# Six FFNs take the second half of x through memory and VectorE and interleave two groups' halves; span levels paired, entry reordered

## What is computed

```python
x = x + 0.5 * swiglu(rmsnorm(x, ffn1_norm), wg, wu, wd)     # D_FF = 2816
h = rmsnorm(x, mix_norm)
x = x + mixing(h @ w_in) @ w_out
x = x + 0.5 * swiglu(rmsnorm(x, ffn2_norm), ...)
...
def swiglu(h, w_gate, w_up, w_down):
    return (jax.nn.silu(h @ w_gate) * (h @ w_up)) @ w_down
```

## Time and profile before

| | |
|---|---|
| median of three runs | 1969.18 us |
| the profiled execution | 1967.95 us |
| its span, first to last instruction | 1966.1 us |
| PE busy | 1953.5 us, 99% |
| DVE busy | 1368.3 us, 70% |
| ACT busy | 1048.3 us, 53% |
| DMA, mean | 202 GB/s |
| matmul records of line 477 with 512 columns | 3 x 1552 and 3 x 832 |
| transposes of x at line 522 | 176 |
| transposes of `act` at line 636 | 68 |
| granted TensorE clock, mean share | 0.999 |

### The profile page before, as it was taken

One profiled execution on the slowest core, in us unless ns is written; L12 is line 12 of the kernel. 1 busy time (PEld: TensorE's weight loads), 2 busy tenths in 40 slices (PEclk: granted clock), 3 DMA queues, 4 the chain that ended last, 5 costly groups with the idle time before them and its releaser, 6 DMA issues.

```text
span 1966.1 us, 27227 instructions
## 1 busy us (share of the span) xinstructions
PE 1953.5 (99%) x11122; PEld 1643.0 (84%) x11122; DVE 1368.3 (70%) x1690; ACT 1048.3 (53%) x1326; POOL 39.5 (2%) x73
## 2 busy tenths in 40 slices
PE   9999999999999999999999999999999999999998
PEld 7888988888888888888888898788888889878887
DVE  6666986666666697666666679766666667976665
ACT  5545675445544657544644466654454446765444
POOL 0120003000000000000000000000000000000000
PEclk9999999999999999999999999999999999999999
DMA  8765546665666544566566644356656664435662
GB/s 321 256 229 193 167 156 217 227 225 193 216 226 225 188 164 169 214 225 218 188 225 228 217 171 160 142 199 225 224 188 235 224 226 161 171 136 194 227 226 78
DMA packets 146749, 396.77 MB, mean 202 GB/s; under 512 B 82128, under 2 KB 100816, under 8 KB 104128
## 3 DMA queue, kind: packets, MB, share of 16 engines
q1 hardware_dynamic: 144704, 390.90, 57.3%
q0 software_dynamic: 1488, 3.78, 0.6%
q10 hardware_dynamic: 432, 0.35, 0.1%
HBM read 372.97 MB, written 19.66 MB: 200 GB/s over the span
## 4 chain that ended last, share of the span: by engine, by line
PE 91%; DVE 5%; ACT 2%; DVEq 1%; issue 1%; DMA 1%; ACTq 0%; SPq 0%
PE bank L477 86%; DVE w_lo L1423 2%; PE bank L522 1%; DMA x<-xt 1%; PE bank L711 1%; PE bank L831 0%; PE bank L727 0%; ACT w_hi L992 0%; PE bank L850 0%; PE bank L636 0%; PE bank L744 0%; PE bank L812 0%; PE bank L700 0%; DVE arena L1561 0%; PE bank L788 0%
## 5 line engine op out<-in xcount | busy, mean ns | idle before, releaser
L1423 DVE TENSOR_TENSOR w_lo<-raw,w_hi 128x2048 fp32r<-128x2048 f32 x330 | 756.2, 2292 | 385.0 <-ACT w_hi L992 384.5
L992 ACT ACTIVATE w_hi<-raw 128x2048 fp32r<-128x2048 f32 x330 | 629.5, 1909 | 247.4 <-PE bank L477 244.9
L477 PE MATMUL bank<-w_hi,h_hi 128*128 128x512 f32 x1552 | 608.5, 392 | 1.9 <-DVE w_lo L1423 1.9
L477 PE MATMUL bank<-w_hi,h_lo 128*128 128x512 f32 x1552 | 604.4, 389 | 0.0
L477 PE MATMUL bank<-w_lo,h_hi 128*128 128x512 f32 x1552 | 604.1, 389 | 0.0
L477 PEld LDWEIGHTS bank<-w_hi,h_hi 128*128 128x128 f32 x1552 | 291.3, 188 | 65.1 <-DVE w_lo L1423 3.2
L477 PEld LDWEIGHTS bank<-w_hi,h_lo 128*128 128x128 f32 x1552 | 291.3, 188 | 61.0
L477 PEld LDWEIGHTS bank<-w_lo,h_hi 128*128 128x128 f32 x1552 | 291.4, 188 | 59.4
L477 PE MATMUL bank<-w_hi,act_hi 128*128 128x512 f32 x832 | 326.8, 393 | 0.0
L477 PE MATMUL bank<-w_hi,act_lo 128*128 128x512 f32 x832 | 324.1, 390 | 0.0
L477 PE MATMUL bank<-w_lo,act_hi 128*128 128x512 f32 x832 | 323.9, 389 | 0.0
(11 more groups left out here) (242 smaller groups left out, 1352.1 us busy)
## 6 DMA issues: line engine op xcount, KB each, us to landing
raw<-stream SPq DMA_DIRECT2D x331, 1024.0 KB, 4.9
spill<-scratch SPq DMA_DIRECT2D x71, 256.0 KB, 3.6
scratch<-spill SPq DMA_DIRECT2D x71, 256.0 KB, 2.7
arena<-arena SPq DMA_DIRECT2D x32, 64.0 KB, 2.7
arena<-rpb POOLq DMA_DIRECT2D x16, 66.5 KB, 4.2
x<-xt SPq DMA_DIRECT2D x1, 1024.0 KB, 12.8
arena<-final_gain POOLq DMA_DIRECT2D x2, 512.0 KB, 5.4
out<-x SPq DMA_DIRECT2D x3, 256.0 KB, 2.5
```

The source lines that it names most:

```text
L477: last = mm(o, a, r, start=start and n == 0, stop=stop and n == len(pairs) - 1)
L992: fn(w_hi[u % SLOTS][:, :], raw[u % RAW][:, :], ACT.Copy).then_inc(hi_done, 1)
L1423: tt(w_lo[u % SLOTS][:, :], raw[u % RAW][:, :], w_hi[u % SLOTS][:, :].bitcast(F32), ALU.subtract).then_inc(lo_done, 1)
```

## The change

It touches the six FFNs other than the first of each model (`SWAPPED`).

- x's second half of columns isn't transposed by PE. When a piece of it is updated, SP writes it to memory (`spill_x`, 256 KB, pieces of 64 columns), waits for both, and reads both back in another order of partitions (`swap_x`). This stands in SP's list behind the raw load of the unit that is five places behind the FFN's first one. DVE transposes 32 x 32 blocks, two instructions of 128 x 256 for each quarter (`x_turn`). The rows of the gate and up weights and of the norm's gain are permuted on the host to match (`swapped_rows`).
- PE's order is front 0, front 1, back 0, first tile of back 1, turn of `act` 0, second tile of back 1, down 0. The stream has places 1 and 2 exchanged for this.
- DVE's order at the entry: updates and h_lo of quarters 0 and 1, split of front 1, sum of squares, split of back 0, two turns of x, h_lo of quarters 2 and 3, splits of places 3 and 4, gates. ACT's: squares and h_hi of quarters 0 and 1, root, split of back 0 and place 3, h_hi of quarters 2 and 3, split of place 4, gates.
- Span levels 0 and 1, and in model 1 also 2 and 3, stand in one slot, the later one, and the second of each pair uses the banks `PD[2:4]` and, for level 3 of model 1, a scaled tile of its own. In model 2 the split of unit 7 moves behind the eviction of unit 5.
- At the kernel's entry quarters 2 and 3 are split together ahead of unit 1, and unit 2 is split in halves.

```diff
+SPANS_AT = [{3: (0, 1), 5: (2, 3), **{t + 2: (t,) for t in range(4, 9)}}, {6: (0, 1), **{t + 5: (t,) for t in range(2, 9)}}]
+SECOND = [(1, 3), (1,)]
+SWAPPED = [(b, L, j) for b in range(2) for L in range(LAYERS) for j in range(2) if (L, j) != (0, 0)]
+SWAPPED_NORMS = [3 * (2 * b + L) + 2 * j for b, L, j in SWAPPED]
...
+        x_landed, x_columns = part(7168, 2, 512), part(8192, 4, T)
-        PS = banks[:, 2:4, :]
+        qks_second = decay_A[:, 0, :, :].rearrange("p (a b) t -> p a b t", a=2)
...
+                if (b, L, j) in SWAPPED and off in (1, 2):
+                    off = 3 - off
...
+        def scaled_tile(b, t):
+
+            return qks2 if b == 1 else qks_second if t == 3 else qks1
+
+        def span_banks(b, t):
+
+            return 4 if t in SECOND[b] else 2
...
+            elif nn in SWAPPED_NORMS and i >= 2:
+                engine.wait_ge(x_turned, 2 * SWAPPED_NORMS.index(nn) + i - 1)
             else:
-                engine.wait_ge(xt_ready, 4 * (nn - 1) + i + 1)
+                engine.wait_ge(xt_ready, sum(2 if m in SWAPPED_NORMS else 4 for m in range(1, nn)) + i + 1)
...
+            if nn in SWAPPED_NORMS and i >= 2:
+                return x_columns[:, 2 * (i - 2) + c, :]
...
+            def swap_x(b, L, j):
+
+                no = SWAPPED.index((b, L, j))
+                for t in range(2):
+                    wait_x(sp, x_no(b, L, 2 * j), 2 + t)
+                    sp.dma_start(spill_x[t].rearrange("c p h -> p c h"), x[:, t, 512:D].rearrange("p (c h) -> p c h", c=8)).then_inc(x_out, 16)
+                sp.wait_ge(x_out, 32 * (no + 1))
+                for t in range(2):
+                    sp.dma_start(x_landed[:, t, :].rearrange("p (q n) -> p q n", q=2),
+                                 spill_x[t].rearrange("(q c) (r a) h -> (c r) q (a h)", q=2, a=4)).then_inc(x_back, 16)
...
-            exchanged = {ffn_use(b, L, j, "front", g) + SLOTS + RAW: (b, L, j, g) for b, L, j, g in EXCHANGED}
+            exchanged = {ffn_use(b, L, j, "back", g) + SLOTS + RAW - 1: (b, L, j, g) for b, L, j, g in EXCHANGED}
+            swapped = {ffn_use(b, L, j, "front", 0) + RAW: (b, L, j) for b, L, j in SWAPPED}
...
+                if u in swapped:
+                    swap_x(*swapped[u])
...
+                if following is not None and nn + 1 not in SWAPPED_NORMS:
...
+                        if g == 0 and kk == 0 and u > 0 and nn not in SWAPPED_NORMS:
...
+                        if t == 0 and between is not None:
+                            between()
...
                 front(PD, 0)
-                back(PD, 0)
-                for g in range(1, GROUPS):
+                if nn in SWAPPED_NORMS:
+                    front(PB, 1)
+                    back(PD, 0)
+                    back(PB, 1, lambda: turn_act(0))
+                    down(0)
+                else:
+                    back(PD, 0)
+                for g in range(2 if nn in SWAPPED_NORMS else 1, GROUPS):
                     front(PB, g)
...
-                if t >= 1:
-                    pe.wait_ge(span_copied, base)
-                src = (qk1, qk2)[b] if kind == "diag" else (qks1, qks2)[b]
+                if t >= 2:
+                    pe.wait_ge(span_copied, base - (t in SECOND[b]))
+                src = (qk1, qk2)[b] if kind == "diag" else scaled_tile(b, t)
...
-                if i in SPAN_AFTER[b]:
-                    span_step(b, L, SPAN_AFTER[b][i])
+                for t in SPANS_AT[b].get(i, ()):
+                    span_step(b, L, t)
...
+                swap = (b, L, j) in SWAPPED
+                if swap:
+                    squares(v, [0, 1])
+                    turned_hi(b, L, 2 * j, [0, 1])
+                    squares(v, [2, 3])
+                    root(v)
+                    split(use_of("back", 0))
+                    split(use_of("front", 0) + SLOTS)
+                    turned_hi(b, L, 2 * j, [2, 3])
+                    split(use_of("front", 1) + SLOTS)
+                elif v > 0:
...
-                    for half in range(2):
-                        turned_hi(b, L, 2 * j, [half + 2])
-                        half_high(1, half)
-                    split(use_of("front", 1))
+                    turned_hi(b, L, 2 * j, [2, 3])
+                    for u in (1, 2):
+                        for half in range(2):
+                            half_high(u, half)
...
-                root(x_no(b, L, 2 * j))
-                if v > 0 and not entry:
-                    split(use_of("front", 1))
+                if not swap:
+                    root(x_no(b, L, 2 * j))
-                if not late:
-                    split(use_of("front", 0) + SLOTS)
...
-                    split(use_of("front", g) + SLOTS)
+                    if not (swap and g == 1):
+                        split(use_of("front", g) + SLOTS)
...
+                def x_turn(b, L, j, q):
+
+                    dve.wait_ge(x_back, 32 * (SWAPPED.index((b, L, j)) + 1))
+                    for t in range(2):
+                        v.transpose(x_columns[:, 2 * q:2 * q + 2, :].rearrange("p k (t r a) -> p t a k r", t=2, a=4)[:, t],
+                                    x_landed[:, t, 256 * q:256 * q + 256].rearrange("p (a k i) -> p a k i", a=4, k=2))
+                    dve.drain().then_inc(x_turned, 1)
...
+                swap = (b, L, j) in SWAPPED
+                if swap:
+                    update(nn - 1, (0.5, 1.0)[j], [0, 1, 2])
+                    turned_lo(b, L, 2 * j, [0])
+                    update(nn - 1, (0.5, 1.0)[j], [3])
+                    turned_lo(b, L, 2 * j, [1])
+                    split(use_of("front", 1))
+                    mean_square(at)
+                    split(use_of("back", 0))
+                    for q in range(2):
+                        x_turn(b, L, j, q)
+                    turned_lo(b, L, 2 * j, [2, 3])
+                    split(use_of("front", 0) + SLOTS)
+                    split(use_of("front", 1) + SLOTS)
...
-                    for half in range(2):
-                        turned_lo(b, L, 2 * j, [half + 2])
-                        half_low(1, half)
-                    split(use_of("front", 1))
+                    turned_lo(b, L, 2 * j, [2, 3])
+                    for u in (1, 2):
+                        for half in range(2):
+                            half_low(u, half)
...
-                if at > 0 and not entry:
-                    split(use_of("front", 1))
                 late = entry or at == 0
-                if not late:
-                    split(use_of("front", 0) + SLOTS)
...
-                    split(use_of("front", g) + SLOTS)
+                    if not (swap and g == 1):
+                        split(use_of("front", g) + SLOTS)
...
-                    tt(qks1.rearrange("p a b t -> p (a b t)"), qk1.rearrange("p a b t -> p (a b t)"),
+                    tt(scaled_tile(0, t).rearrange("p a b t -> p (a b t)"), qk1.rearrange("p a b t -> p (a b t)"),
...
-                src = PS[:, :, 0:T].rearrange("p o (n t) -> p o n t", t=64)
+                at = span_banks(b, t)
+                src = banks[:, at:at + 2, 0:T].rearrange("p o (n t) -> p o n t", t=64)
...
-                split(mix_use(1, L, 7))
...
+                    if b == 1 and i == 5:
+                        split(mix_use(1, L, 7))
...
-                    if t < len(STEPS) and not (b == 0 and i == RECURRENCE_AFTER[b]):
-                        span_copy(b, L, t)
+                    if not (b == 0 and i == RECURRENCE_AFTER[b]):
+                        for done in SPANS_AT[b].get(i, ()):
+                            span_copy(b, L, done)
...
+def swapped_rows(w):
+
+    half = w[512:].reshape(2, 4, 2, 32, -1).transpose(0, 2, 1, 3, 4).reshape(512, -1)
+    return np.concatenate([w[:512], half], 0)
...
+                if (b, L, j) in SWAPPED:
+                    g, u = ([swapped_rows(w[L])] * LAYERS for w in (g, u))
+                at = len(out)
...
+                if (b, L, j) in SWAPPED:
+                    out[at + 1], out[at + 2] = out[at + 2], out[at + 1]
...
+            norms = [i[n + tail][L].reshape(D, 1) for n in ("ffn1_norm", "mix_norm", "ffn2_norm")]
+            norms = [swapped_rows(w) if (b, L, n // 2) in SWAPPED and n != 1 else w for n, w in enumerate(norms)]
```

More of the change, by code:

```diff
@@ L88, in build @@
 def build(nc, stream, xt, x_cols, params, final_gain, code_w, gate_w, forget_w, rpb,
-          lower, positions, forget_bias, c_square, c_level, c_col, c_att, c_freq, c_sel, c_reset, spill, out):
+          lower, positions, forget_bias, c_square, c_level, c_col, c_att, c_freq, c_sel, c_reset, spill, spill_x, out):
     ctx = ExitStack()
@@ L538, in last_row_unit @@
                         turn(nn + 1, x, 0, 1)
-                if following is not None:
+                if following is not None and nn + 1 not in SWAPPED_NORMS:
                     wait_x(pe, following, 2)
@@ L617, in front, with back @@
                     last.then_inc(used, 1)
-                def back(banks, g):
```

(12 more changed lines are left out.)

11 lines of the change are left out of this document (5 added, 6 removed).

## The result

The changed kernel takes 1972.05 us (median of 21 runs, 1971.26 to 1973.85), the kernel before 1969.01 in 21 runs beside it: ratio 1.0017, 95% interval 1.0010 to 1.0023. That is +3.0 us where +0.6 was forecast: inside the range and inside the 0.2% (3.9 us) called no change, but the interval leaves out 1, so the kernel is slower, by 0.10 to 0.23%. The direction of the forecast (what is gained is spent on a new wait) stands; its size is 2.4 us short.

The account below looks back on a forecast made before the run. PE's issue rate bounds the kernel (busy 1953.5 of 1966.1 us). Six FFN entries +1.8, paired span levels -1.2, model 2's pairs 0 and the kernel's entry 0 make +0.6 on 1969.18: 1969.8 us, range 1965.3 to 1976.

Parts of the forecast that it names:

- The transposes ahead of front 0: FFN entries: this group takes 0.49 us but only fills the wait for h_lo; priced at nothing, bound 0.08 us.
- Those inside front 0, 0.43 us: FFN entries: removing the four transposes inside the first unit gains 0.35 us plus 0.08 of restart.
- The chain to back 0: FFN entry: root 789.94, w_lo 792.61 to 794.81, x's columns 793.9; DVE's order, not the DMAs, sets the time.
- ACT's h_hi ... is ready at 796.85, so DVE makes h_lo from 797.07: FFN entry, after the turn: h_lo ready 797.95, PE starts 798.1, waiting 0.7 us ahead of back 0.
- net +0.3 us at each entry: Six FFN entries: back 0 ends at 803.6 instead of 803.30; six times gives +1.8 us.
- The five other entries that the change touches show the same pattern, within 0.1 us: FFN entries: the one starting at 786.40 stands for all six, so one price is taken six times.
- act_lo of group 0 with 0.6 us to spare: Ahead of the first down unit: ready 808.9, wanted 809.5, nothing added; rival that it is late, +9.6 us, chance 0.08.
- Pairs: Mixings: joining span levels saves 0.3 us a pair, -1.2 in model 1, 0 in model 2; giving-nothing rival's chance 0.15.
- So the saving stays: Mixings of model 1: DVE's results are in time, so the -1.2 us is kept; bound, none of it.
- the first that could be late: Mixing of model 1: the next slots' probabilities, ready at 246.29, wanted at 247.21, 0.9 us to spare.
- Kernel's entry, 0: Reordered entry of the whole kernel: the chain to place 3's w_lo, where PE waits 1.7 us, is untouched: 0.
- The rival of late columns: FFN entries: x's columns land up to 2.5 us late; halfway, 1.2 late each, +7.2 on the forecast, 1977; chance 0.14.

Follow-up runs that it names:

- no_first: Kernel before without the four transposes of x ahead of front 0 at the six entries, nothing in their place: 1969.01 us, ratio 1.0002.
- no_turns: Kernel before without any of the eight transposes of x's second half at the six entries, nothing in their place: 1966.47 us, ratio 0.9990.
- early_split: Changed kernel with ACT's split of back 0's weights moved ahead of the root: 1966.86 us, ratio 0.9991 against the kernel before.
- returns_twice: Changed kernel with both returns issued once more ahead of the real ones, so x's columns land later: 1980.92 us, ratio 1.0063 against the kernel before.
- gpsimd_later: Changed kernel with GpSimd's 16 additions (position bias of mixing 1.2) held back by 49 us: 1970.87 us, ratio 1.0012 against the kernel before.
- swap_only: Changed kernel with span levels one to a slot again, as before: 1973.09 us, ratio 1.0021 against the kernel before.
- pairs_only: Kernel before with the paired span levels alone: 1967.64 us, ratio 0.9994.
- entry_only: Kernel before with the reordered entry of the whole kernel alone: 1968.54 us, ratio 1.0001.
- after: The changed kernel itself, as profiled: median 1972.05 us, ratio 1.0017 against the kernel before.
- early_both: early_split with x's first-half transposes in two groups, behind piece 1's matmuls and in the middle of piece 2's: 1967.76 us, ratio 0.9993 against the kernel before.
- own_returns: early_old_entry with each return waiting for its own spill alone and DVE turning the first piece's blocks first: 1962.70 us, ratio 0.9972 against the kernel before.
- early_old_entry: early_both with the kernel's old entry and DVE's first h_lo ahead of the update of piece 2: 1965.41 us, ratio 0.9984 against the kernel before.
- own_returns_later: own_returns with GpSimd's 16 additions held back as in gpsimd_later: 1961.66 us, ratio 0.9967 against the kernel before.

## Why the prediction was right, and where it was off

Its times for the entry are taken in the clock of the earlier trace rows; 1.52 us are subtracted from those of the changed kernel.

- **The transposes ahead of front 0 are worth nothing: right.** The start stays 0.14 us behind h_lo (786.90 + 0.88 to 787.92), no_first gains nothing, and the wait that they had filled is now listed.
- **Those inside front 0, 0.43 us: right.** no_turns shows 0.45 to 0.48 at five entries.
- **The chain to back 0: right up to the turn, at this entry.** Root 789.94 forecast and measured, w_lo of back 0 792.61 forecast and measured, turn 794.81 and 794.82, front 1's end 797.38 and 797.40. The columns: 793.9 forecast, 793.81 measured; it was ACT's and DVE's order that set the time, as early_split and returns_twice show from both sides. That the columns were met within 0.1 us is partly luck: over the six entries they landed 5.97 to 7.83 us behind the issue of the second spill, and this entry, with 6.93, is in the middle.
- **The term that was mis-sized is what follows, "ACT's h_hi ... is ready at 796.85, so DVE makes h_lo from 797.07", and with it "net +0.3 us at each entry".** Two turns with their drains hold DVE 0.16 us longer (797.23), so the wait is 0.86 instead of 0.7 and the entry +0.5 instead of +0.3 (the turns are 0.16 of these 0.2 us, the rest is rounding). Ahead of back 0 the six waits come to 5.8 us by the distance of starts, where about 4 was forecast. Six times 0.2 is 1.2 us.
- **"The five other entries that the change touches show the same pattern, within 0.1 us" was no ground for one price at all six.** In the kernel before, GpSimd's additions lay beside the entry of the second FFN of layer 1.1 too, in front of work that had room. The new order puts two of the lengthened DVE instructions on PE's path: +0.6 us more there, shown by gpsimd_later.
- **act_lo of group 0 with 0.6 us to spare: right.** No wait stands ahead of down 0; act_lo is ready at 810.74 and PE comes to down 0 at 811.28, so 0.5 us were left.
- **Pairs: direction right, size too large.** Alone, they give 0.47 and 0.40 us in a mixing of model 1 instead of 0.6, and nothing in model 2, by the wait that was named. In the changed kernel model 1 gives only 0.15 and 0.51. "So the saving stays" failed in mixing 1.1: at 255.34 PE waits 0.3 us for probabilities from DVE, the kind of result that the prediction had named as the first that could be late, but 8 us behind the ones whose times it had checked. Mixing 2.2 takes 0.3 us more; that comes with the swap (swap_only has it, pairs_only doesn't), as a longer wait for the probabilities. Why they are later there is open.
- **Kernel's entry, 0: right for the median of entry_only.** The half clock in some executions was not foreseen; in the changed kernel it is worth about 0.3 us of the median.
- **What the terms make.** The profiled pair differs by 3.9 us, 3.3 more than the +0.6: 1.9 at the six entries, 0.9 in the mixings, 0.5 in the first FFN. The 2.4 us between the medians can't be divided as closely, since the two profiled executions don't stand at the same distance from their medians.

The rival of late columns was nearer than its chance of 0.14 says. At the last entry of the changed kernel the second return took 4.85 us and the columns were there only 0.1 us before DVE.

## What to carry to other kernels

Before work is moved off the bound engine, ask what it waits for at the place where the work stood: transposes that fill a wait are free. A new path through memory and two engines needs the order of the helpers' instructions rewritten around it, one consumer at a time: here the same change is +3.0 us with ACT's root ahead of a split that DVE waits for, -2.1 with the two exchanged, and -5.9 with the next two waits (ahead of front 0, and for the returns) taken in turn and the kernel's old entry back. Where a pattern is laid over several places, look at every engine at each of them, the idle-looking one too.

## What was not expected of the hardware

- GpSimd's additions of 128x128 lengthen DVE's instruction of 2.29 us by 0.26, in no_turns by 1.4, and one of 0.15 to 0.39. The addition that meets a split takes 2.48 us instead of 0.43.
- Two returns of 256 KB side by side land 2.7 to 2.8 and 3.0 to 3.1 us after issue at the four entries of the changed kernel outside layer 2.2; four, at the entry shown, 2.8, 3.1, 4.2 and 4.4, and the last of them 4.3 to 6.6 at the other five. At those two entries of layer 2.2 the second return took 4.3 to 4.9 us in six profiles (after, swap_only, early_split, early_both, gpsimd_later, own_returns) and 3.7 to 4.0 in two (early_old_entry, own_returns_later); the cause is open.
- After 3.36 us without work (3.5 by the distance of starts) PE restarted at its full clock of 2.4 GHz, and 0.8 us later ran at 1.2 GHz for 3.4 us, with matmuls 0.427 us apart instead of 0.227, in returns_twice (windows as above):

```profile
1302.00:1304.00 2.00, 2.00 (x7) 1.58 (x7) 2.00 (x3) 1.98 (x2) 0.00 (x0) 0.63 0.02 8
1304.00:1306.00 2.00, 2.00 (x6) 1.51 (x6) 2.00 (x2) 0.68 (x1) 0.00 (x0) 0.52 0.23 33
1306.00:1308.00 2.00, 2.00 (x10) 1.62 (x9) 1.86 (x3) 0.47 (x1) 0.00 (x0) 1.00 0.81 332
```

That adds 1.6 us (eight matmuls, 0.2 each) to the 2.7 us by which this wait had grown. The other five entries of that kernel, with waits of 1.7 to 2.1 us by the distance of starts, kept their clock.
